# The later adaptive-modulation weights: scaled and summed in pairs on GpSimd, so that TensorE runs half as many matmuls on them

## The reference

```python
def first_block(x, c, positions, w_ada, b_ada, ...):
    c_act = jax.nn.silu(c)                      # 1 x 1024
    ada = c_act @ w_ada[l] + b_ada[l]           # 1024 x 6144 weights
    sh_m, sc_m, g_m, sh_f, sc_f, g_f = jnp.split(ada, N_ADA, axis=-1)
    h = modulate(rmsnorm(x, norm_mix_g[l]), sh_m, sc_m)
    mix = hybrid_mixer(h, ...)                  # MLA and forgetting attention, gated
    x = x + g_m[:, None, :] * mix
    h = modulate(rmsnorm(x, norm_ffn_g[l]), sh_f, sc_f)
    x = x + g_f[:, None, :] * conv_ffn(h, ...)
    return rmsnorm(x, norm_final_g)
```

## Time and profile before

| | |
|---|---|
| median of 3 runs | 1103.9 us (1099.53 to 1108.15) |
| the profiled execution's own time | 1107.4 us |
| its span in the profile | 1105.1 us |
| granted TensorE clock, mean over the span | 0.966 |
| busy: PE, DVE, ACT, POOL | 92%, 40%, 35%, 2% |

### The profile page before, as it was taken

How to read it: one execution, slowest core, us unless ns; L and a number is a source line. 1 busy time by engine, 2 the same in 40 slices (tenths; PEclk the granted TensorE clock), 3 DMA queues, 4 the chain that set the end, 5 groups by cost and what they waited for, 6 DMA issues and landing times.

```text
span 1105.1 us, 15393 instructions
## 1 busy us (share of the span) xinstructions
PE 1012.3 (92%) x6226; PEld 677.7 (61%) x6226; DVE 445.3 (40%) x830; ACT 389.6 (35%) x675; POOL 23.6 (2%) x50
## 2 busy tenths in 40 slices
PE   2799889999899999979889799999999999999999
PEld 1498777888799999958879633434343434343433
DVE  1553466657688568666574511011111011111111
ACT  0343455554566456444543320303030303031302
POOL 1000000000000000012001000000000000000000
PEclk9799999999899999989899699999999999999999
DMA  9664864284354655624724589799999999999994
GB/s 333 250 222 149 325 246 153 77 303 156 114 192 174 208 158 186 220 86 158 298 77 158 224 317 421 295 423 423 422 423 421 424 421 423 422 422 423 422 422 195
DMA packets 81577, 309.06 MB, mean 280 GB/s; under 512 B 6738, under 2 KB 32376, under 8 KB 54904
## 3 DMA queue, kind: packets, MB, share of 16 engines
q1 hardware_dynamic: 78744, 307.17, 71.1%
q10 hardware_dynamic: 2784, 1.21, 0.4%
HBM read 307.31 MB, written 1.05 MB: 279 GB/s over the span
## 4 chain that ended last, share of the span: by engine, by line
PE 47%; DVE 2%; ACT 1%; issue 1%; ACTq 0%; DVEq 0%
PE ps L948 45%; DVE wc L2094 1%; PE ps L1422 1%; ACT wc L937 1%; PE ps L1344 0%; PE ps L1396 0%; DVE wb L1910 0%; PE ps L1275 0%; DVE wa L1901 0%; DVE wl L1463 0%; DVE wb L1932 0%; ACT wh L586 0%; DVE wa L1855 0%; PE ps L1264 0%; DVE aL L1860 0%
## 5 line engine op out<-in xcount | busy, mean ns | idle before, releaser
L1463 DVE TENSOR_TENSOR wl<-ring,wh 128x1024 fp32r<-128x1024 f32 (+4 forms) x156 | 184.3, 1192 | 127.2 <-ACT wh L586 126.9
L586 ACT ACTIVATE wh<-ring 128x1024 fp32r<-128x1024 f32 (+4 forms) x156 | 159.9, 1033 | 156.0 <-PE ps L948 121.2
L948 PE MATMUL ps<-hH,wh 128*128 128x256 f32 x704 | 202.4, 287 | 6.0 <-DVE hL L1489 1.9
L948 PE MATMUL ps<-hL,wh 128*128 128x256 f32 x704 | 200.0, 284 | 0.0
L948 PE MATMUL ps<-hH,wl 128*128 128x256 f32 x704 | 199.7, 284 | 0.0
L948 PE MATMUL ps<-slot,xT 128*64 128x512 f32 x384 | 167.9, 593 | 0.0
L948 PE MATMUL ps<-ring,xT 128*64 128x512 f32 x512 | 167.8, 594 | 0.0
L948 PEld LDWEIGHTS ps<-hH,wh 128*128 128x128 f32 x704 | 135.5, 192 | 10.3 <-issue 5.6
L948 PEld LDWEIGHTS ps<-hH,wl 128*128 128x128 f32 x704 | 135.3, 192 | 0.0
L948 PEld LDWEIGHTS ps<-hL,wh 128*128 128x128 f32 x704 | 135.3, 192 | 0.0
L948 PE MATMUL ps<-work,wc 128*64 128x512 f32 x512 | 113.4, 595 | 11.0 <-ACT wc L937 11.0
(11 more groups left out here) (310 smaller groups left out, 1220.3 us busy)
## 6 DMA issues: line engine op xcount, KB each, us to landing
work<-w_exp_down SPq DMA_DIRECT2D x64, 1024.0 KB, 13.1
ring<-w_exp_up SPq DMA_DIRECT2D x32, 1024.0 KB, 11.1
ring<-w_exp_gate SPq DMA_DIRECT2D x32, 1024.0 KB, 18.1
slot<-w_exp_up SPq DMA_DIRECT2D x32, 1024.0 KB, 13.1
ring<-w_ada SPq DMA_DIRECT2D x12, 2048.0 KB, 9.7
ring<-w_in SPq DMA_DIRECT2D x12, 2048.0 KB, 8.5
ring<-w_up SPq DMA_DIRECT2D x22, 1024.0 KB, 7.3
slot<-w_exp_gate SPq DMA_DIRECT2D x8, 2048.0 KB, 20.8
```

The lines of the kernel that those rows point to most:

```text
L586: nc.scalar.activation(wh[:, c % CHUNKS, 0:n], src, ACT.Copy).then_inc(S("chunk_high"), 1)
L948: return nc.tensor.matmul(o_, l, r, start=start, stop=stop, skip_group_check=True)
L1463: V.tensor_tensor(wl[:, c % CHUNKS, 0:n], src, wh[:, c % CHUNKS, 0:n].bitcast(F32), ALU.subtract)\
```

## The change

GpSimd gets a new step `ada_pair`. For each of the eight later items it waits until the item has landed, and then works in two halves of 1024 columns: it multiplies each of the two K-tiles by its column of `cact`, in place (two `tensor_scalar` of 128 x 1024), waits for both on its own semaphore, and adds the second to the first, in place (one `tensor_tensor` of 128 x 1024). `ada_part` keeps its place on PE; for the later eight it no longer waits for the load but for the sums, and makes four matmuls instead of eight, with a column of ones. The first four items (third 0) stay as they were.

```diff
@@ gpsimd @@
+            def ada_pair(third, i):
+
+                it = IT[f"ada{third}{i}"]
+                pool.wait_ge(S(f"slot{it['slot']}_loaded"), it["loaded"])
+                w = slot_view(it)
+                for h in range(2):
+                    c0 = 1024 * h
+                    n = 2 * (4 * third - 4 + i) + h + 1
+                    for kk in range(2):
+                        v = w[:, kk, c0:c0 + 1024]
+                        nc.gpsimd.tensor_scalar(v, v, cact[:, 2 * i + kk:2 * i + kk + 1], None, ALU.mult).then_inc(S("ada_product"), 1)
+                    pool.wait_ge(S("ada_product"), 2 * n)
+                    nc.gpsimd.tensor_tensor(w[:, 0, c0:c0 + 1024], w[:, 0, c0:c0 + 1024], w[:, 1, c0:c0 + 1024], ALU.add)\
+                        .then_inc(S("ada_summed"), 1)
+
             power("norm", TT, 1)
+            pool.wait_ge(S("c_steps"), 2)
+            ada_pair(1, 0)
             power("lat", 4)
+            for i in range(1, 4):
+                ada_pair(1, i)
+            for i in range(4):
+                ada_pair(2, i)
             power("norm", TT, 2)
@@ tensor, ada_part @@
                 it = IT[f"ada{third}{i}"]
+                w = slot_view(it)
+                if third:
+                    for q in range(4):
+                        pe.wait_ge(S("ada_summed"), 2 * (4 * third - 4 + i) + q // 2 + 1)
+                        ins = mm(ps[32 * q:32 * q + 1, 7, :], ones[:, 0:1], w[:, 0, 512 * q:512 * q + 512], i == 0, i == 3)
+                    ins.then_inc(S("ada_used"), 1)
+                    return
                 pe.wait_ge(S(f"slot{it['slot']}_loaded"), it["loaded"])
-                w = slot_view(it)
```

## The result

| | before | after |
|---|---|---|
| median | 1106.0 us (1099.5 to 1112.3, 4 runs) | 1137.2 us (1135.1 to 1139.0, 4 runs) |
| profiled execution, span | 1105.1 us | 1136.9 us |
| granted TensorE clock | 0.966 | 0.958 |

The ratio is 1.0282 (95% interval 1.0217 to 1.0347), +31 us. The forecast was 1114 us with a range to 1127.

What follows compares the result with a forecast made beforehand. PE, busy 92% of the span, was taken as the bound, with loads also setting the pace in the first block. -6.0 + 0.5 + 6.5 + 9 = +10.0 us, against the median of 1103.9 gave 1114 us; range 1097 to 1127.

Steps and rivals of the forecast that it cites:

- POOL's side: what an item costs: POOL's price per item: multiplies 1.1 us, adds 2.0, waits 0.4, together 8.8 us; bounds 5.8 to 12.
- rival D: POOL itself becomes the bound: item 12.4 us, ada13, ada20 and loads late; +17, 1121 us; chance 0.12.
- Does PE wait for POOL?: Landing plus 8.8 us against PE's use: ada11 in time by 1.4, ada13 late, g0 about 1.3 us late.
- -6.0 us of savings: PE's shorter items in the first block: 0.97 us each, seven saving 0.86; bounds 0 and -6.9.
- +0.5 up to ada13: DVE's splits held up by POOL before ada13, seldom the chunk PE wants next: +0.5 us (0 to 2).
- +6.5 in the rotary stretch: 135.66 to 143.9 us: ada20's six POOL instructions get between DVE's 18; +6.5 us with ada13's lateness (0 to 11).
- +9 in attention: ada21, 22 and 23 on POOL hold up DVE in the attention steps, about 3 us an item: +9 (0 to 20).
- the three terms: POOL and DVE holding each other up: +0.5 up to ada13, +6.5 in the rotary stretch, +9 in attention.
- One to one behind 228 us: Later stages have fixed work, so a shift at the end of attention, near 228 us, reaches the end one to one.

Runs made afterwards that it cites:

- e5: The changed kernel, but POOL multiplies by the constant 0.5 instead of by a column of `cact`: 1129.2 us in one run.
- e4: The changed kernel, but POOL sums only the second 1024 columns of each later item, PE multiplies the first half as before: 1110.6 us, 1.0019 of the kernel before.
- e8: The changed kernel without POOL's work: PE makes four matmuls an item on unscaled weights, second K-tile left out: 1104.4 us, 0.9966 of the kernel before.
- e6: The changed kernel, but each multiply has two inputs, the second `cact` broadcast along the columns: 1150.4 us, 1.0386 of the kernel before.
- e12: The changed kernel with one multiply per half, by the ratio of `cact`'s columns, and ada13 left on PE: 1117.4 us, 1.0099 of the kernel before.
- e2: The changed kernel, but POOL sums only ada10 to ada13; ada20 to ada23 as in the kernel before: 1124.5 us, 1.0168 of that kernel.
- e10: The changed kernel, but POOL sums only ada11 and ada13; PE multiplies the other six as before: 1127.3 us, 1.0191 of the kernel before.
- e1: The changed kernel, but POOL sums only ada20 to ada23; ada10 to ada13 as in the kernel before: 1113.9 us, 1.0069 of that kernel.
- e7: The changed kernel, but POOL sums only ada12, ada21, ada22 and ada23; PE multiplies the others as before: 1107.3 us, 1.0012 of the kernel before.
- e3: The changed kernel, but POOL does its 48 instructions on spare tiles nobody reads; PE works as before the change: 1116.0 us, 1.0094 of the kernel before.
- e9: The changed kernel, but ada20 is multiplied by PE as before; the other seven stay on POOL: 1133.6 us, 1.0245 of the kernel before.

## Why the prediction was wrong

The sign of the middle forecast (+10 us) was right, its size was not, and 1137 us lies outside the range, which ended at 1127. In part the sign was luck: most of the +31 is lateness of the middle third, which the forecast put at some 3 us. Step by step:

- **What failed: the price of a multiply in "POOL's side: what an item costs".** It was put near the memset, at 1.1 us; it takes 2.83 alone and 3.4 beside DVE. This is above its upper bound of 2.0 as well, which came from the select: the rows had no multiply of a wide tile, and an operation that they lack was bounded by others that only looked alike. The add at 2.0 was nearly right (2.34). The item became 16.0 us for 8.8, beyond the 12.4 of rival D. The Trainium skill's figure for the add (GPSIMD Engine Reference, § 3.1; an estimate of 2.2 us) agrees with 2.34; its "roughly line-rate" for one-input operations (§ 4.1) doesn't agree with the 2.83, nor with the 2.75 of e5's multiply by a constant. Why a multiply costs this on POOL no run shows.
- **What followed: "Does PE wait for POOL?"** The sum's form was right, landing plus item. With 16.0 it gives 94.0 for ada11, 5.8 us over what PE wants (89.06 less 0.9). PE waited 5.08, both sides being later by then: PE came at 91.66, and POOL began ada11 at 78.53, 3 us behind its landing (68.0 + 7.5), because it was still at ada10 and the latents' power. The form left this queue on POOL out. ada10, which it left out too, was late by 3.80, and the three add up through the ring. Where the prediction had one wait of some 3 us, PE waited 19.5 us in four. Rival D's mechanism, POOL as the bound with ada20 and g1 loaded late, is what happened, at a larger price than D's; only its lateness of ada20 itself did not come, since PE was late by more (it reached ada20 at 175.54, POOL was done at 175.0). e4, with an item of 8.0 us in place of the assumed 8.8, shows the forecast's world: no wait, and +2 us by the ratio, not +10.
- **-6.0 us of savings: not told apart from what e8 measured.** 0.97 us an item was right to the hundredth; e8 gets 3.8 (0.2 to 7 by its interval). Its trace shows where less arrives than was summed: nothing up to the first scores, with g0's load and a lower clock taking it back. In the changed kernel late items save nothing: from 146.65 to 148.45 two matmuls of ada13, four records, cost 1.80 us at the lower clock, as much as eight matmuls did at the full one.
- **+0.5 up to ada13: within its bounds.** The term was for DVE held up alone, and what shows of it is one new wait of PE for a split, 1.13 us at 66.89 (up to 2.0 in e6 and e12). What was wrong by far in this stretch is the lateness above: e2 and e10 reach their first scores 19 and 20 us later than before. About 17 of these are waits. A part of the rest is the clock, a term that the forecast didn't have: ukv1 took 1.9 us longer behind the 8.59 us of pause. No run takes the clock away by itself.
- **+6.5 in the rotary stretch, ada13's lateness included: mis-sized by that lateness.** ada20's own part is about 6 us (2 to 10), by e1 against e7. The reason given was half right: behind a multiply DVE waits 0.85 us and not the whole of it, but the multiplies last longer. ada13's lateness, 1.3 us at g0 and 2.8 in the loads there, became 10.6 us of waits and 21.2 in the loads, in which ada10's and ada11's lateness stands as well.
- **+9 in attention: too large.** Its length grew by 2.3 us, and by 5.2 in e1; with the 1.8 that e8 saves there added back, 4.1 and 7.0. In e3, which has no savings, it grew by 3.7. All holding-up together is 9 to 10 us (e3), where the three terms made 16.
- **One to one behind 228 us: held** (+29.1 there, +32.1 at q2 and +33.3 at the end, counted from T0, which itself came 1.5 earlier); the 3 us more up to q2 come in part from PE's pause behind ada23, 1.94 us for 1.08. The parts of middle and last third (18 + 7) leave some 5 us of the 31, less than their intervals together leave uncertain. Single executions also differ by 5 us in the last 620 us of any kernel here: e3 and e1 take 616, before 620 and e8 621. Whether the two thirds simply add up stays open.

What the forecast named as the cost, holding-up less savings, was +6 us by e3 and e8 (10 less 4). The other 25 or so, a difference and not a measurement, are left for what came late and for the clock behind it.

## What to carry to other kernels

Work given to an idle engine is judged by its latency against the slack between landing and use of each piece, and not by the engine's free time: two of eight items carried two thirds of the loss, four with room cost nothing that the runs could tell (at most 4 us). The slack is also eaten by the piece ahead of it on the same engine. An operation that the trace lacks should be timed by itself before it is relied on, and bounded well beyond its look-alikes until then. And compute first what remains if the other engine were free: here it was about 4 us, less than the 9 to 10 that GpSimd and DVE cost each other.

## What the runs showed that I had not expected

- A GpSimd multiply of 128 x 1024 float32 by one scale per partition takes 2.83 us, by a constant 2.75; the same product with the scale as a broadcast second input takes 1.87, and an add of two tiles 2.34.
- GpSimd's one-input multiply keeps DVE out for only 0.85 us of its 2.83, its two-input instructions until they end (DVE's 0.18 us became 2.40 in e6). So the faster form was the worse one: e6 stands at 1.0386 of before, the change at 1.0282.
- A pause can cost PE more than its length, and how much varies. Behind ada11's wait the clock was at 1.2 GHz for 3.7 us after a pause of 5.08 us (the change), but for three windows of 8 us with PE at work after one of 6.41 (e9), and for 13 us after one of 3.27 (e6, 96.9 to 110.2). What decides between these no run shows.
